# PEER decoder block: head 2's query weights loaded in the output stage, and the last norm's gamma and beta brought as two rows and spread by TensorE and ScalarE

## What is computed

```python
h = layer_norm(DN_ALPHA * h + merged @ w_out, ln1_g, ln1_b)
q = (h @ w_q_peer).reshape(n, 8, 2, 128)               # 8 heads, two sides each
s = einsum('nhpc,pkc->nhpk', q, sub_keys)              # 128 keys on each side
sv, si = top_k(s, 16)
...                                                    # best 16 of 16 x 16 pairs: experts, gates
u = u_table[experts]                                   # 128 rows of 2048 for each token
act = gelu(einsum('nd,nhkd->nhk', h, u)) * gates
out = einsum('nhk,nhkd->nd', act, v_table[experts])
h = layer_norm(DN_ALPHA * h + out, ln2_g, ln2_b)
```

## Time and profile before

| | us |
|---|---|
| median of 3 runs (2484.09 to 2484.73) | 2484.39 |
| the profiled execution | 2484.73 |
| its span | 2482.8 |

### The profile page before, as it was taken

How to read it: one execution, slowest core, us unless ns; L and a number is a source line. 1 busy time by engine, 2 the same in 40 slices (tenths; PEclk the granted TensorE clock), 3 DMA queues, 4 the chain that set the end, 5 groups by cost and what they waited for, 6 DMA issues and landing times.

```text
span 2482.8 us, 39170 instructions
## 1 busy us (share of the span) xinstructions
PE 2182.9 (88%) x16085; PEld 1530.2 (62%) x16085; DVE 1529.8 (62%) x2570; ACT 716.3 (29%) x1357; POOL 667.6 (27%) x541
## 2 busy tenths in 40 slices
PE   6999999999999999998998888977777787777776
PEld 5999999999989999986644444532233232322222
DVE  7677787777765555456955666677445544444445
ACT  4555555555434444432211111111001000000000
POOL 1000000000000000001555445555554455444442
PEclk9999999999999999999999999999999999999999
DMA  5433333333347666484999999999999999999997
GB/s 194 130 91 86 103 91 86 103 90 86 95 120 214 186 185 183 135 284 181 420 421 423 422 427 426 403 427 427 428 427 427 426 427 427 427 428 427 427 427 311
DMA packets 346497, 710.34 MB, mean 286 GB/s; under 512 B 13832, under 2 KB 270400, under 8 KB 279744
## 3 DMA queue, kind: packets, MB, share of 16 engines
q0 software_dynamic: 74176, 537.01, 51.4%
q1 hardware_dynamic: 271904, 170.62, 23.1%
q10 hardware_dynamic: 240, 0.21, 0.0%
HBM read 705.69 MB, written 2.10 MB: 285 GB/s over the span
## 4 chain that ended last, share of the span: by engine, by line
DMA 32%; PE 16%; DVE 2%; issue 2%; POOL 1%; DVEq 0%; ACT 0%; POOLq 0%; ACTq 0%
DMA down_rows<-in_v_table,experts 29%; PE bank L1573 13%; DMA up_rows<-in_u_table,experts 3%; PE bank L1522 2%; POOL down_rows L1510 0%; POOL up_rows L1504 0%; DVE up_rows L1674 0%; PE bank L1544 0%; PE bank L1532 0%; ACT diagonal L1626 0%; PE bank L1538 0%; DVE one_hot L1210 0%; DVE expert_sides L1216 0%; DVE side_index L1189 0%; DVE side_index L1182 0%
## 5 line engine op out<-in xcount | busy, mean ns | idle before, releaser
L1573 PE MATMUL bank<-down_rows,diagonal 128*128 128x512 f32 x2032 | 947.2, 610 | 224.2 <-DMA down_rows<-in_v_table,experts 188.6
L1674 DVE CUSTOM_DVE_ANT_0 up_rows<-up_rows,h 128x2048 f32<-128x2048 f32 x256 | 585.4, 2291 | 537.2 <-DMA up_rows<-in_u_table,experts 537.2
L1573 PEld LDWEIGHTS bank<-down_rows,diagonal 128*128 128x128 f32 x2032 | 374.8, 192 | 752.9 <-issue 378.1
L1504 POOL DMA_INDIRECT up_rows<-in_u_table,experts x256 | 287.5, 1123 | 1192.7 <-POOLq L1228 1098.6
L1510 POOL DMA_INDIRECT down_rows<-in_v_table,experts x256 | 371.6, 1452 | 551.1 <-PE bank L1573 542.0
L180 DVE TENSOR_TENSOR w_half_rest<-w_half,w_half_high 128x1024 fp32r<-128x1024 f32 x224 | 273.0, 1220 | 186.5 <-ACT w_half_high L159 184.7
L195 PE MATMUL project<-hT_high,w_half_high 128*128 128x272 f32 (+1 forms) x1152 | 353.7, 307 | 2.7 <-PEq L202 1.4
L195 PE MATMUL project<-hT_high,w_half_rest 128*128 128x272 f32 (+1 forms) x1152 | 330.7, 287 | 0.0
L195 PE MATMUL project<-hT,w_half_high 128*128 128x272 f32 (+1 forms) x1152 | 330.1, 287 | 0.0
L159 ACT CAST w_half_high<-w_half 128x1024 fp32r<-128x1024 f32 x224 | 234.2, 1049 | 194.5 <-PE merge_ps L195 122.2
L195 PEld LDWEIGHTS project<-hT_high,w_half_high 128*128 128x128 f32 x1152 | 216.9, 188 | 12.3 <-issue 1.6
(11 more groups left out here) (314 smaller groups left out, 2979.4 us busy)
## 6 DMA issues: line engine op xcount, KB each, us to landing
w_half<-in_w_in SPq DMA_DIRECT2D x176, 512.0 KB, 3.8
w_half<-in_w_branch_a SPq DMA_DIRECT2D x32, 512.0 KB, 3.9
out_w<-in_w_out SPq DMA_DIRECT2D x16, 1024.0 KB, 5.2
query_w<-in_w_q_peer SPq DMA_DIRECT2D x10, 1024.0 KB, 32.9
w_half<-in_w_branch_b SPq DMA_DIRECT2D x16, 512.0 KB, 4.0
out_w<-in_w_q_peer SPq DMA_DIRECT2D x6, 1024.0 KB, 36.0
up_rows<-in_u_table,experts POOLq DMA_INDIRECT x256, 16.2
down_rows<-in_v_table,experts POOLq DMA_INDIRECT x256, 15.6
```

Source lines behind the costliest of these rows:

```text
L1504: pool.indirect_dma_start(ur[n % RU][:], None, w["u_table"][0], bass.IndirectOffsetOnAxis(ap=k.idx[:, t, h, j:j + 1], axis=0)).then_inc(s_ ...
L1573: mm = nc.tensor.matmul(acc[t][c][:], dg[n % RD][:], vr[n % RV][:, quarter(c)], start=False, stop=(n == last(t, c)), skip_group_check=True)
L1674: v.tensor_tensor_reduce(ur[n % RU][:], ur[n % RU][:], k.h[:, n // (HEADS * TOPK), :], 1.0, 0.0, ALU.mult, ALU.add, dots[:, n:n + 1]).then ...
```

## The change

Head 2's query weights get their buffer (third, the same query_w2) among the routing buffers, which exist in out_stage too, and SP loads them there, behind quarters 11 and 13. In the expert stage SP's loop starts at head 3. To make room, only identity and the row 0 to 15 are kept to the end (k.kept, 144 columns); the other constants and the vectors of the first stages are freed with them.

The last norm's gamma and beta come as two rows of 8 KB into partitions 0 and 1 of the third buffer's second half (rows), once the last head that uses this buffer (head 5) is projected. At the end of units 24 and 28 PE multiplies each row by a 2 x 128 selector of ones (pick), four matmuls of 512 columns into the four late banks, and in its passes 28 and 32 ACT copies the four banks to gamma and then to beta. PE's opening of tile 1 and DVE's finish(0) wait for these copies.

```diff
@@ -41,10 +41,9 @@
 LEVELS = 6
 
 
-C_ID, C_ONES, C_SCAN, C_SU, C_IU, C_M1, C_IST = 0, 128, 256, 576, 640, 704, 768
-C_LEV = 832
-C_IOTA = C_LEV + 64 * LEVELS
-C_CEN = C_IOTA + 16
+C_ID, C_IOTA, NKEPT = 0, 128, 144
+C_ONES, C_SCAN, C_SU, C_IU, C_M1, C_IST, C_LEV = 0, 128, 448, 512, 576, 640, 704
+C_CEN = C_LEV + 64 * LEVELS
 C_BLK = C_CEN + 64
 NCONST = C_BLK + 2
 HALF = CH // 2
...
 
 
 
@@ -125,6 +125,8 @@
         query = self.sb("query_w0", [P, KT, 2 * P])
         self.query_w = [[query[:, 0:KT // 2, :], query[:, KT // 2:KT, :]]]
         self.query_w += [[x[:].rearrange("p a (b c) -> p (a b) c", c=2 * P) for x in self.out_raw]]
+        self.third = self.sb("query_w2", [P, KT, 2 * P])
+        self.query_w += [[self.third[:, 0:KT // 2, :], self.third[:, KT // 2:KT, :]]]
         self.sc, self.sc2 = self.sb("scores", [P, TT, 2, N_KEYS]), self.sb("scores_left", [P, 2, N_KEYS])
         self.sv, self.si, self.sif = self.sb("side_best", [P, 2, TOPK]), self.sb("side_index", [P, 2, TOPK], U32), self.sb("side_index_f", [P, 2, TOPK])
         self.cand, self.cand2 = self.sb("candidates", [P, TOPK, TOPK]), self.sb("candidates_left", [P, TOPK * TOPK])
@@ -218,7 +220,7 @@
         s_turn, s_meta_ev, s_ev, s_hT = k.sem("in_turned"), k.sem("in_meta_evacuated"), k.sem("in_evacuated"), k.sem("in_hT")
         s_w, s_wround, s_wsplit = [k.sem(f"lora_w{g}") for g in range(4)], k.sem("lora_rounded"), k.sem("lora_split")
         s_mm, s_own, s_mix, s_wide = k.sem("lora_projected"), k.sem("lora_own"), k.sem("lora_mixed"), k.sem("in_gamma_beta")
-        ident = k.const[:, C_ID:C_ID + P]
+        ident = k.kept[:, C_ID:C_ID + P]
         tiles = [(xm, META), (k.h[:, 0, :], P), (k.h[:, 1, :], P)]
         ORDER4 = (2, 3, 0, 1)
         QK = KT // 4
@@ -233,7 +235,7 @@
                 sp.dma_start(lraw[:, QK * g:QK * g + QK, :], src[:, QK * g:QK * g + QK, LORA0:POOL0]).then_inc(s_w[g], 16)
             for g in range(3):
                 k.load_half(sp, g)
-            sp.dma_start(k.const[:, P:NCONST], w["consts"][:, P:NCONST]).then_inc(s_const, 16)
+            sp.dma_start(k.const[:], w["consts"][:, NKEPT:NKEPT + NCONST]).then_inc(s_const, 16)
             for n, (dst, g) in enumerate(((gam, "ln_in_g"), (bet, "ln_in_b"))):
                 sp.wait_ge(s_hT, 4 * n + 5)
                 sp.dma_start(dst, row_broadcast(w[g])).then_inc(s_wide, 16)
@@ -308,7 +310,7 @@
         @block.scalar
         def _(act):
             act.dma_start(xm, w["meta_tokens"]).then_inc(s_meta, 16)
-            act.dma_start(k.const[:, 0:P], w["consts"][:, 0:P]).then_inc(s_id, 16)
+            act.dma_start(k.kept[:], w["consts"][:, 0:NKEPT]).then_inc(s_id, 16)
             for n, g in enumerate(("ln_in_g", "ln_in_b")):
                 act.dma_start(gb_raw[n * KT:(n + 1) * KT, :], w[g].rearrange("(r c) -> r c", c=P)).then_inc(s_gb_raw, 16)
 
@@ -1208,7 +1210,7 @@
     v.tensor_copy(pf[:], pij[:])
     d()
     v.tensor_tensor(hot[:], pf[:].rearrange("p i (n a) -> p (i n) a", a=1).to_broadcast((P, 2 * TOPK, TOPK)),
-                    k.const[:, C_IOTA:C_IOTA + TOPK].rearrange("p (a n) -> p a n", a=1).to_broadcast((P, 2 * TOPK, TOPK)), ALU.is_equal)
+                    k.kept[:, C_IOTA:C_IOTA + TOPK].rearrange("p (a n) -> p a n", a=1).to_broadcast((P, 2 * TOPK, TOPK)), ALU.is_equal)
     d()
     for i in range(2):
         v.tensor_tensor(hot[:, i], hot[:, i], sif[:, i, :].rearrange("p (a n) -> p a n", a=1).to_broadcast((P, TOPK, TOPK)), ALU.mult)
@@ -1252,6 +1254,8 @@
                     sp.dma_start(dst[:], row_broadcast(w[src][0])).then_inc(k.s_gb, 16)
                 if g in (7, 8):
                     k.load_query(sp, w, 0, g - 7)
+                if g in (11, 13):
+                    k.load_query(sp, w, 2, g // 2 - 5)
             for i in range(2):
                 sp.wait_ge(s_split, QUARTERS - 1 + i)
                 k.load_query(sp, w, 1, i)
@@ -1439,9 +1443,8 @@
         dots, weights = sb("dots", [P, SLOTS]), sb("weights", [P, SLOTS])
         aid = sb("alpha_identity", [P, P])
         gam, bet, stats, mv, rs = k.gam, k.bet, k.stats, k.mv, k.rs
-        third = sb("query_w2", [P, KT, 2 * P])
-        k.query_w += [[third[:, 0:KT // 2, :], third[:, KT // 2:KT, :]]]
-        y = third[:, 0:KT // 2, :].rearrange("p k c -> p (k c)")
+        y, rows = (k.third[:, i * KT // 2:(i + 1) * KT // 2, :].rearrange("p k c -> p (k c)") for i in range(2))
+        pick = sb("row_of_two", [2, 2, P])
         acc0, late = k.bank[0:4], k.bank[4:8]
         acc, pq, pk = (acc0, late), late[0:2], late[2:4]
         s_tp, s_tc, s_h = k.sem("peer_turn"), k.sem("peer_turned"), k.sem("ln1_second")
@@ -1452,8 +1455,10 @@
         s_v = [k.sem(f"down_arrived{i}") for i in range(RV)]
         s_dot, s_gelu, s_weight, s_diag, s_added = k.sem("peer_dot"), k.sem("peer_gelu"), k.sem("peer_weight"), k.sem("peer_diag"), k.sem("peer_added")
         s_tail = k.sem("peer_tail")
-        s_aid, s_gb, s_var, s_root, s_norm, s_out = k.sem("peer_aid"), k.sem("peer_gb"), k.sem("peer_var"), k.sem("peer_root"), k.sem("peer_norm"), k.sem("peer_out")
-        ident = k.const[:, C_ID:C_ID + P]
+        s_pick, s_row, s_wide = k.sem("row_pick"), k.sem("ln2_row"), k.sem("ln2_wide")
+        WIDE_MM, WIDE_COPY = (PER_TILE - 8, PER_TILE - 4), (PER_TILE - 4, PER_TILE)
+        s_aid, s_gb, s_var, s_root, s_norm, s_out = k.sem("peer_aid"), k.sem("ln2_rows"), k.sem("peer_var"), k.sem("peer_root"), k.sem("peer_norm"), k.sem("peer_out")
+        ident = k.kept[:, C_ID:C_ID + P]
 
         def behind(u):
 
@@ -1477,13 +1482,13 @@
 
         @block.sync
         def _(sp):
-            for h in range(2, HEADS):
-                wait(sp, s_qmm, 2 * (h - 3) + 2)
+            for h in range(3, HEADS):
+                sp.wait_ge(s_qmm, 2 * (h - 3) + 2)
                 for i in range(2):
                     k.load_query(sp, w, h, i)
-            sp.wait_ge(s_h, 4)
-            sp.dma_start(gam[:], row_broadcast(w["ln2_g"][0])).then_inc(s_gb, 16)
-            sp.dma_start(bet[:], row_broadcast(w["ln2_b"][0])).then_inc(s_gb, 16)
+            sp.wait_ge(s_qmm, 2 * max(range(2, HEADS, 3)) + 2)
+            for i, n in enumerate(("ln2_g", "ln2_b")):
+                sp.dma_start(rows[i:i + 1, :], w[n]).then_inc(s_gb, 16)
             for t in range(TT):
                 for i, c in enumerate(WRITE[t]):
                     sp.wait_ge(s_norm, 4 * t + i + 1)
@@ -1537,6 +1542,18 @@
                 for n in range(4):
                     nc.tensor.matmul(acc[t][n][:], aid[:], k.h[:, t, n * 512:(n + 1) * 512], start=True, stop=False, skip_group_check=True)
 
+            def widen(i):
+
+                if i == 0:
+                    pe.wait_ge(s_gb, 32)
+                    pe.wait_ge(s_pick, 2)
+                    pe.wait_ge(s_q, 2 * HEADS)
+                    pe.wait_ge(s_s, 2 * HEADS)
+                else:
+                    pe.wait_ge(s_wide, 4)
+                for c in range(4):
+                    nc.tensor.matmul(late[c][:], pick[:, i, :], rows[0:2, quarter(c)], start=True, stop=True).then_inc(s_row, 1)
+
             def second_query(q4):
                 pe.wait_ge(s_tc, q4 + 1)
                 for kt in range(4 * q4, 4 * q4 + 4):
@@ -1561,8 +1578,7 @@
             score(1)
             for u in range(UNITS):
                 if u == PER_TILE:
-                    pe.wait_ge(s_q, 2 * HEADS)
-                    pe.wait_ge(s_s, 2 * HEADS)
+                    pe.wait_ge(s_wide, 8)
                     begin(1)
                 for i in range(UNIT):
                     n = UNIT * u + i
@@ -1583,6 +1599,8 @@
                         query(h, n - UNIT, TOPK - UNIT)
                     elif h < HEADS:
                         query(h, n % TOPK, TOPK)
+                if u in WIDE_MM:
+                    widen(WIDE_MM.index(u))
                 h, r = divmod(u - PER_HEAD - 1, PER_HEAD)
                 if r == 0 and 2 <= h + AHEAD < HEADS:
                     score(h + AHEAD)
@@ -1648,6 +1666,11 @@
                     scores(1, 1)
                 if u >= CLOSER:
                     diagonal(u)
+                if u in WIDE_COPY:
+                    i = WIDE_COPY.index(u)
+                    for c in range(4):
+                        act.wait_ge(s_row, 4 * i + c + 1)
+                        nc.scalar.copy((gam, bet)[i][:, quarter(c)], late[c][:]).then_inc(s_wide, 1)
                 if u == PER_TILE + 4:
                     root(0)
                 if r == 3 and g + 2 < HEADS:
@@ -1659,6 +1682,8 @@
         def _(dve):
             v, d = nc.vector, nc.vector.drain
             v.tensor_scalar(aid[:], ident, ALPHA, None, ALU.mult).then_inc(s_aid, 1)
+            for i in range(2):
+                v.tensor_copy(pick[:, i, :], ident[0:2, i:i + 1].to_broadcast((2, P))).then_inc(s_pick, 1)
 
             def gate(h, t):
 
@@ -1693,7 +1718,7 @@
 
                 if part == 0:
                     dve.wait_ge(s_added, HEADS * TOPK)
-                    dve.wait_ge(s_gb, 32)
```

(21 more changed lines are left out.)

## The result

| kernel | us, median (lowest to highest) | profiled execution, its span | ratio to before (95%) |
|---|---|---|---|
| before | 2484.39 (2483.54 to 2485.08) | 2484.73, 2482.8 | |
| after | 2497.12 (2495.8 to 2498.92) | 2497.12, 2495.2 | 1.0051 (1.004 to 1.0063) |

What follows compares the result with a forecast made beforehand. The expert stage was taken as bound by DMA transfers at about 427 GB/s. From 2484.4 us, -5.0 (head 2) -4.9 (gamma, beta) +0.8 (front) +1.5 (output stage) +0.2 (widening) +0.2 (copies) gave 2477.2, range 2474.0 to 2482.5.

Steps and rivals of the forecast that it cites:

- The part on the constants: Kernel start: the identity's load grows from 64 to 72 KB, taken as 0, at most 0.3 us.
- Head 2's weights: Expert stage: 2.10 MB less to move saves 5.0 us; 2.7 after the front loss and the output stage's hold.
- The front loss: Start of the expert stage: without head 2's halves the DMA engines get less work, 0 to 1.5 us lost, 0.8 taken.
- Output stage: Head 2's loads delay later weight loads and splits 14 and 15, holding PE: 1.5 us taken, bounds 0 and 3.4.
- Gamma and beta: Expert stage: two 8 KB rows replace two 1.05 MB spreads, 4.9 us saved; 4.5 after widening and two small copies.
- The rate around the widenings: Units 24 to 32: PE's added matmuls and ACT's copies cost 0.2 us in all, between 0 and 1.
- The gather near 1260: Early expert stage: this GpSimd gather lands in about 12 us instead of 16.8.
- A DMA share under 0.98 between 1160 and 1260: Sign at the front of the expert stage that would make the forecast wrong.
- the 359 GB/s stretch: Dip at 1560 to 1580, 3.2 us lost; expected to stay, moved by some 8 us; used for the one-half rival.
- Slower (about 2497): Rival: PE waits ahead of begin(1) for ACT's copies, up to one unit of 19.6 us without DMA; chance 0.06.
- Nothing: Rival: the loads' time was idle of others, or their bytes aren't taken out; 2484.4 us, chance 0.03.
- one half: Rival: head 2's gap idles DMA as long as its loads kept it busy, 5 us not regained; 2482, chance 0.16.

Runs made afterwards that it cites:

- experiment 1: The changed kernel with 64 unused bytes a partition ahead of h1T, so buffers from there on start at multiples of 256: 2476.86 us, ratio 0.9969 to before.
- experiment 11: The kernel before with 256 unused bytes a partition ahead of the gathered rows, which still start at a multiple of 256: 2484.24 us, ratio 1.0 to before.
- experiment 5: The changed kernel moved by the same 64 bytes, with head 2's query weights loaded at the front of the expert stage again: 2480.07 us, ratio 0.9983 to before.
- experiment 6: The changed kernel moved by the same 64 bytes, with gamma and beta spread by DMA as before, without widening: 2481.56 us, ratio 0.9988 to before.

## Why the prediction was wrong, point by point

- **What bounds the expert stage.** Right: gathered bytes at the engines' rate, and bytes taken out are worth their time, once the rate is kept. What failed is the step behind it: "eight gathered rows of 1 MiB, so 2.45 us each" was read in before and carried into after as if it were a constant of the chip. It is one of this kernel's layout, 2.49 us at 192 past the boundary. The part on the constants costed only the identity's load; that a smaller table moves every buffer behind it was given no price. That missing term is +20.3 us (experiment 1); the other terms came out at -7.9 in experiment 1's runs (before 2484.72 there), forecast -7.2.
- **Head 2's weights.** 3.2 us for 2.7. The front loss was 1.3 by the first 20 us and 1.7 by the first 100, around its upper bound of 1.5.
- **Output stage.** The late steps were as forecast, the hold smaller. The view of waits of the changed kernel, 1060 to 1135, has the hold as one line:

```profile
PE bank L197 <- DVE out_w_rest L182: 0.6, 1, 0.6
```

  The evacuation of tile 0 starts at 1134.52, 1.9 us later than 1132.58 before; SP's first out_w load of the stage was already 0.7 late (1054.72 for 1054.04), which is not the change's hold. Between 0.6 and 1.3 us remain, for 1.5 taken. In experiment 1, from that load to the evacuation, it is 78.8 us for 78.5: 0.3.
- **Gamma and beta.** 4.7 for 4.5. The rate around the widenings cost 0.5 to 2.3 us, where the sum had 0.2 and a bound of 1: this term was sized too small. What made up for it is open. The estimate of half a microsecond for a transfer to two partitions, from the Trainium skill ("SBUF — State Buffer", section "Door 1: The DMA port swizzle"), can't be told apart in any run: the traces have no landing time for the two rows.
- **The signs.** Three of my own were bad. The gather near 1260 was to land in 12 us: it took 17.81, and 17.13 in experiment 1, where the gain is there. What failed is the step that takes 2 MiB off the wait of this very gather. GpSimd is paced by PE's slots up to there, as forecast, but SP's own next loads moved up in head 2's place (SP free at 1244.3 for 1259.4), and the gain shows only in the issue times of later gathers. A DMA share under 0.98 between 1160 and 1260 was to refute the forecast: over the whole it is 0.99 in the changed kernel and in experiment 1, but 0.83 and 0.87 in 1160 to 1180, so by its first part the sign would have refuted a gain that is there. And the 359 GB/s stretch isn't a trait of the kernel: experiment 1 has 423 there, and experiment 11, before's own code 256 bytes further on, equals before in time without the dip: 425 in the slice of its page where rows 1 has 403. It can't carry the price of a rival.
- **The rivals.** "Slower (about 2497)" hit the number by accident. Its mechanism, PE waiting ahead of begin(1), is absent (no idle there at 1863.29), and 20.3 us spread over all units is another thing than one unit lost. "Nothing" and "one half" are refuted by experiments 1, 5 and 6.

## What to carry to other kernels

Where transfers set the pace, read the first byte of each destination buffer before and after an edit, even an edit far from them: any tile that shrinks or goes moves what is allocated behind it. Keep buffers that a saturated queue writes at a multiple of 256 bytes in a partition; a pad tile does it. When a calm stretch far from the edit has another GB/s at the same DMA share, look at the layout before the queues.

## What the runs showed of the hardware

- Rows of 8 KB gathered to a start that is no multiple of 256 bytes move at 421 GB/s for 427 (419 at an offset of 32), with both streams off; with one off, at 426 (2000 to 2400 us). The share of busy DMA time is 1.01 in all of these stretches: it doesn't see this.
- The price doesn't grow with the offset: 19.1 us at 128, 19.2 at 192, 23.4 at 32, none at 256 (2484.24 for 2484.69).
- Two streams off cost 19.2 us; down rows (with what lies behind them) alone 6.2, up rows alone 4.2. Why is open.
